# A two-layer hybrid decoder trunk: hardware loops written out, weights split ahead across the layer border, no norm prepared in the last layer, output in four blocks

## The reference

```python
for l in range(DEPTH):
    h = rms_norm(x, norm1_g[l])
    proj = h @ w_in[l]
    q, k, v, iq, ik, iw, glu_in, mq, gates = jnp.split(proj, bounds, axis=-1)
    ...
    y_attn = dsa_sparse_attention(q, k, v, iq, ik, iw) @ w_attn_o[l]
    ...
    y_mem = memory_cross_attention(mq, mk, mv) @ w_mem_o[l]
    y_conv = conformer_conv(...) @ w_conv_o[l] + conv_o_b[l]
    g = jax.nn.sigmoid(gates + gate_b[l]).reshape(B, S, N_BRANCH, D_MODEL)
    merged = g[:, :, 0] * y_attn + g[:, :, 1] * y_mem + g[:, :, 2] * y_conv
    x = x + merged @ w_out[l]
    h2 = rms_norm(x, norm2_g[l])
    x = x + jnp.square(jax.nn.relu(h2 @ w_up[l])) @ w_down[l]
return x
```

## Time and profile before

| | |
|---|---|
| median of three runs | 2966.69 us |
| the profiled execution | 2967.76 us |
| its span | 2966.1 us |
| TensorE busy | 2891.1 us |
| VectorE busy | 1745.2 us |
| ScalarE busy | 1347.8 us |
| GpSimd busy | 313.6 us |
| HBM read, written | 550.37 MB, 6.29 MB |
| mean granted TensorE clock | 0.996 of full speed |

### The profile page before, as it was taken

How to read it: one execution, slowest core, us unless ns; L and a number is a source line. 1 busy time by engine, 2 the same in 40 slices (tenths; PEclk the granted TensorE clock), 3 DMA queues, 4 the chain that set the end, 5 groups by cost and what they waited for, 6 DMA issues and landing times.

```text
span 2966.1 us, 38416 instructions
## 1 busy us (share of the span) xinstructions
PE 2891.1 (97%) x13120; PEld 2376.0 (80%) x13120; DVE 1745.2 (59%) x1849; ACT 1347.8 (45%) x1657; POOL 313.6 (11%) x331
## 2 busy tenths in 40 slices
PE   7998999999999999999999989999999999999998
PEld 6876788888888888888878768888888888888887
DVE  4689655556555555545546986555555555555554
ACT  5543644444443444444445446444444434344443
POOL 1158200000000000000020772000000000000000
PEclk9999999999999999999999999999999999999999
DMA  7653556665656556565565444666566565555653
GB/s 268 203 167 128 157 181 202 206 219 199 199 185 198 185 187 195 184 189 188 185 225 171 163 141 154 188 208 231 185 203 201 188 189 186 195 184 186 196 185 128
DMA packets 274090, 558.65 MB, mean 188 GB/s; under 512 B 13168, under 2 KB 13168, under 8 KB 271376
## 3 DMA queue, kind: packets, MB, share of 16 engines
q1 hardware_dynamic: 266384, 523.53, 53.8%
q0 software_dynamic: 5888, 30.02, 3.6%
q10 hardware_dynamic: 1664, 3.15, 0.3%
HBM read 550.37 MB, written 6.29 MB: 188 GB/s over the span
## 4 chain that ended last, share of the span: by engine, by line
PE 88%; DVE 5%; issue 4%; DMA 1%; ACT 1%; DVEq 0%; ACTq 0%; POOL 0%; POOLq 0%; SPq 0%
PE acc L548 28%; PE acc L550 28%; PE acc L549 28%; DVE conv_acc L1152 3%; PE tp L561 3%; DVE lo L1091 1%; ACT hi L818 1%; PE tp L631 1%; DMA conv_bias<-in_conv_o_b 1%; PE sc L615 0%; PE sc L604 0%; DVE index L1170 0%; DMA x_tok<-in_x 0%; DMA raw<-in_w_in 0%; DVE head_sum L1278 0%
## 5 line engine op out<-in xcount | busy, mean ns | idle before, releaser
L1091 DVE TENSOR_TENSOR lo<-raw,hi 128x1024 fp32r<-128x1024 f32 (+1 forms) x1008 | 1239.5, 1232 | 1172.4 <-ACT hi L818 1163.6
L818 ACT ACTIVATE hi<-raw 128x1024 fp32r<-128x1024 f32 (+1 forms) x1008 | 1055.6, 1048 | 1472.3 <-PE acc L550 1468.3
L548 PE MATMUL acc<-hi,hT_hi 128*128 128x512 f32 x2304 | 922.4, 400 | 37.3 <-DVE lo L1091 37.2
L550 PE MATMUL acc<-hi,hT_lo 128*128 128x512 f32 x2304 | 902.2, 392 | 0.0
L549 PE MATMUL acc<-lo,hT_hi 128*128 128x512 f32 x2304 | 901.2, 391 | 0.0
L548 PE MATMUL acc<-hi,bT_hi 128*128 128x512 f32 x1408 | 555.3, 394 | 0.0
L550 PE MATMUL acc<-hi,bT_lo 128*128 128x512 f32 x1408 | 548.9, 390 | 0.0
L549 PE MATMUL acc<-lo,bT_hi 128*128 128x512 f32 x1408 | 548.2, 389 | 0.0
L548 PEld LDWEIGHTS acc<-hi,hT_hi 128*128 128x128 f32 x2304 | 434.8, 189 | 135.6 <-DVE lo L1091 48.5
L550 PEld LDWEIGHTS acc<-hi,hT_lo 128*128 128x128 f32 x2304 | 434.6, 189 | 93.8
L549 PEld LDWEIGHTS acc<-lo,hT_hi 128*128 128x128 f32 x2304 | 435.1, 189 | 86.7
(11 more groups left out here) (224 smaller groups left out, 1641.1 us busy)
## 6 DMA issues: line engine op xcount, KB each, us to landing
raw<-in_w_in SPq DMA_DIRECT2D x160, 1024.0 KB, 5.0
raw<-in_w_up SPq DMA_DIRECT2D x128, 1024.0 KB, 5.3
raw<-in_w_down SPq DMA_DIRECT2D x128, 1024.0 KB, 5.1
raw<-in_w_out SPq DMA_DIRECT2D x32, 1024.0 KB, 5.1
raw<-in_w_mem_kv SPq DMA_DIRECT2D x16, 1024.0 KB, 5.1
raw<-in_w_attn_o SPq DMA_DIRECT2D x16, 1024.0 KB, 5.1
raw<-in_w_conv_o SPq DMA_DIRECT2D x8, 1024.0 KB, 5.0
raw<-in_w_mem_o SPq DMA_DIRECT2D x8, 1024.0 KB, 5.1
```

What stands on the lines that cost most here:

```text
L548: pe.matmul(o, a1, w1, start=first and dk == 0, stop=False)
L550: mm = pe.matmul(o, a2, w1, start=False, stop=last and dk == 1)
L818: act.activation(hi[:, u % 4, :, 0:w], raw[:, c, 2 * (u % 2):2 * (u % 2) + 2, 0:w], ACT.Copy).then_inc(hi_ready, 1)
L1091: dve.tensor_tensor(lo[:, u % 4, :, 0:w], raw[:, u // 2, 2 * (u % 2):2 * (u % 2) + 2, 0:w], hi[:, u % 4, :, 0:w].bitcast(F32), ALU.subtrac ...
```

## The change

1. Every hardware loop of the five engines is written out by the Python program. Wait values become constants; `Place` loses `base` and `loop`.
2. At the layer border VectorE no longer adds block 3 of x at the end of the layer; it adds and scales it after unit 3 of the next layer's front (n == 3), after four splits.
3. In the last layer `mlp` gets `last` as false for its last quarter too, so blocks 0 to 2 are not scaled, squared, transposed and split, and GpSimd doesn't load the gain for it.
4. The output goes in four DMAs of 512 channels, each as soon as its block is added.

```diff
-PER = {
-    "layer": {"group": GROUPS, "unit": GROUPS * UNITS, "acc0": 35, "acc1": 35, "fill": 112, "tp0": 56, "tp1": 56,
...
+A_LAYER = {"group": GROUPS, "unit": GROUPS * UNITS, "acc0": 35, "acc1": 35, "fill": 112, "tp0": 56, "tp1": 56,
...
     def now(self, name):
-        return self.base[name] + self.n[name]
+        return self.n[name]
...
-    @contextmanager
-    def loop(self, kind, i, first, trips):
...
+    def layer_done(self):
+
+        for name, per in A_LAYER.items():
+            if name not in self.counted:
+                self.n[name] += per
...
             sp.wait_ge(x_in[1], 16)
-            with sp.Fori(0, LAYERS) as l, here.loop("layer", l, 0, LAYERS):
+            for l in range(LAYERS):
...
-                with sp.Fori(0, CB) as cb, here.loop("merge", cb, 0, CB):
+                for cb in range(CB):
...
-                with sp.Fori(0, FFN // D) as qu, here.loop("ffn", qu, 0, FFN // D):
+                for qu in range(FFN // D):
...
-            sp.wait_ge(x_new, LAYERS * (CB + CB * FFN // D))
-            sp.dma_start(out_tokens.rearrange("t p d -> p t d"), x_tok[:, :, :]).then_inc(out_done, 16)
-            sp.wait_ge(out_done, 16)
+            for b in range(CB):
+                cols = slice(b * COL, (b + 1) * COL)
+                sp.wait_ge(x_new, LAYERS * (CB + CB * FFN // D) - CB + b + 1)
+                sp.dma_start(out_tokens.rearrange("t p d -> p t d")[:, :, cols], x_tok[:, :, cols]).then_inc(out_done, 16)
+            sp.wait_ge(out_done, 16 * CB)
...
@@ TensorE @@
-            with pe.Fori(0, LAYERS) as l, here.loop("layer", l, 0, LAYERS):
+            for l in range(LAYERS):
...
-                mlp(True, False)
-                with pe.Fori(1, FFN // D - 1) as qu, here.loop("ffn", qu, 1, FFN // D - 2):
-                    mlp(False, False)
-                mlp(False, True)
+                for qu in range(FFN // D):
+                    mlp(qu == 0, qu == FFN // D - 1 and l < LAYERS - 1)
+                here.layer_done()
...
@@ VectorE (ScalarE's loops are written out in the same way) @@
-            with dve.Fori(0, LAYERS) as l, here.loop("layer", l, 0, LAYERS):
+            for l in range(LAYERS):
+                layer_fill[0] = here.now("fill")
                 origin[0] = here.now("unit")
                 for n in range(FRONT * UNITS):
                     split(n % UNITS, width_of(n // UNITS))
-                    if n == 0:
+                    if n == 0 and l == 0:
+                        scale_block(CB - 1)
+                    if n == 3 and l > 0:
+                        add_block(CB - 1, 0, -1)
                         scale_block(CB - 1)
                     side(n)
...
-                mlp(False, True)
-                origin[0] = here.now("unit")
-                add_block(CB - 1, 0, -1)
+                    mlp(qu == 0, qu == FFN // D - 1 and l < LAYERS - 1)
                 here.next("rstd_ready", 2)
+                here.layer_done()
+            origin[0] = here.now("unit")
+            add_block(CB - 1, 0, -1)
...
@@ GpSimd @@
-                pool.wait_ge(scaled, here.next("scaled", T + CB))
-                alone()
-                pool.dma_start(gain[:, :], rows(norm1_g[LAYERS - 1 - l])).then_inc(gain_in, 16)
-                here.next("scaled", CB - 1)
-
-            pool.wait_ge(gain_in, here.now("gain_in"))
+                if l < LAYERS - 1:
+                    pool.wait_ge(scaled, here.next("scaled", T + CB))
+                    alone()
+                    pool.dma_start(gain[:, :], rows(norm1_g[l + 1])).then_inc(gain_in, 16)
+                    here.next("scaled", CB - 1)
+                here.layer_done()
```

More of the change, by code:

```diff
@@ L18 @@
-from contextlib import ExitStack, contextmanager
+from contextlib import ExitStack
 import numpy as np
@@ L784, in _ @@
                 merge(True)
-                with pe.Fori(1, CB) as c, here.loop("merge", c, 1, CB - 1):
+                for c in range(1, CB):
                     merge(False)
@@ L1043, in _ @@
                     take_norm(b, t)
-            with act.Fori(0, LAYERS) as l, here.loop("layer", l, 0, LAYERS):
+            for l in range(LAYERS):
                 origin[0] = here.now("unit")
@@ L1049, in _ @@
                 merge(True, 0)
-                with act.Fori(1, CB) as c, here.loop("merge", c, 1, CB - 1):
+                for c in range(1, CB):
                     merge(False, c)
@@ L1433, in _ @@
                 alone()
-                with dve.Fori(1, CB) as c, here.loop("merge", c, 1, CB - 1):
+                for c in range(1, CB):
                     origin[0] = here.now("unit")
@@ L1621, in _ @@
             here.next("scaled", CB - 1)
-            with pool.Fori(0, LAYERS) as l, here.loop("layer", l, 0, LAYERS):
+            for l in range(LAYERS):
                 pool.wait_ge(squared, here.now("squared") + T * CB)
@@ L1639, in _ @@
                         biases(l, 0)
-                with pool.Fori(1, CB) as c, here.loop("merge", c, 1, CB - 1):
+                for c in range(1, CB):
                     pool.wait_ge(bias_used, here.next("bias_used"))
```

66 lines of the change are left out of this document (20 added, 46 removed).

## The result

| | before | after |
|---|---|---|
| median | 2966.48 us (2966.23 to 2967.82, 4 runs) | 2942.98 us (2941.28 to 2944.02, 4 runs) |
| the profiled execution | 2967.76 us | 2942.02 us |
| its span | 2966.1 us | 2940.2 us |

The ratio is 0.9918, with a 95% interval of 0.9903 to 0.9933: 23.5 us faster, and the profiled executions lie 25.7 us apart. The forecast was 16.9 us and 2949.8 us, with a range down to 2946.0.

A forecast was written before the change was run, and what follows sets the result against it. TensorE, busy 97% of the span, was taken to bound the kernel. Terms 5.8 + 2.4 + 1.3 + 2.8 + 3.4 + 1.2 = 16.9 us took the median from 2966.69 to 2949.8 us, range 2946.0 to 2953.8.

The forecast's parts named there:

- Layer border, gap and clock: Between layers 0 and 1: moving VectorE's add removes TensorE's gap, 5.8 us, and the low clock behind it, 2.4 us.
- Start: Before the first matmul: ScalarE's activation table load moves to the first tanh, saving 1.3 us, bounds 0 and 1.3.
- Last layer without the norm: TensorE's last quarter: six groups of four transposes go, saving 2.8 us, bounds 2.6 and 2.9.
- Output: After the last add: only a 512 KB transfer of 3.0 us remains, saving 3.4 us, bounds 1.4 and 4.0.
- Registers gone: Mainly VectorE in the front: constant wait values shorten starts behind the top-k, saving 1.2 us, bounds 0 and 3.5.
- 0.06, times 16: VectorE in the front: 0.06 us kept per `lo` start after top-k replacement, times 16, giving 1.0 us.
- The 2 us for the clock: In the front: one clock fall more or less, 2 us either way, as part of the range.
- 1, the gap only moved: Layer border: late add and scale delay transposes or parked x, 8.2 us come back, giving 2958.0 us; 5%.
- 2, instruction supply: TensorE's longer list: instruction packets come too slowly; at 0.3 us each, 13 us slower, 2979.8 us; 3%.
- 3, little changes: Whole kernel: the border gap comes back and two more clock falls occur, saving 4.7 us, giving 2962.0 us; 2%.
- a wait for `xg`: Near the layer border: a TensorE wait for `xg` would show a forecast error.
- a pitch above 0.227: In the MLP: a pitch above 0.227 would show a forecast error.

The follow-up runs named there:

- e1: Kernel before with only VectorE's loops written out, the last x block's add left at the layer's end: 2955.66 us (before, same chip: 2967.16).
- e12: Kernel after, but VectorE's add of the last x block back at the end of layer 0, the scale after the first split: 2946.64 us.
- e2: Kernel before with only GpSimd's loops written out: 2965.17 us (before, same chip: 2967.16).
- e4: Kernel before with only the output sent in four blocks, all loops kept: 2964.07 us (before, same chip: 2967.16).
- e3: Kernel before with only ScalarE's loops written out: 2967.57 us (before, same chip: 2967.16).
- e10: Kernel after with six more semaphore increments on GpSimd, once per layer before its first convolution step: 2941.22 us.
- e11: Kernel after with one more semaphore increment on VectorE, once per layer before the first top-k round: 2941.13 us.
- e14: Kernel after, unchanged, measured again on another chip: 2940.91 us over 4 runs, ratio 0.9908 to the kernel before.
- e9: Kernel after with two more semaphore increments on GpSimd, once per layer before its first convolution step: 2941.58 us.
- e7: Kernel before with 29 of GpSimd's 30 multiply-and-add convolution steps left out: 2937.47 us (before, same chip: 2968.68).
- e8: Kernel after with 29 of GpSimd's 30 multiply-and-add convolution steps left out: 2918.50 us.
- e13: Kernel after with GpSimd's 30 convolution multiplications per layer moved to ScalarE, six buffers between: 2941.39 us over 4 runs, ratio 0.9910 to the kernel before.
- e16: Kernel after with 29 of GpSimd's 30 convolution multiplications left out, all additions kept: 2944.19 us.
- e5: Kernel after with one more semaphore increment on VectorE behind each of the eight top-k rounds: 2949.48 us.

## Why the prediction was right and wrong

**Layer border, gap and clock (5.8 + 2.4): right.** 8.1 us for 8.2. Nothing waits for the late scale, and the clock stays at 1.00. e1 and e12 split it: 5.2 by VectorE's loop written out, 2.9 by the order (4.4 with the fall in e12).

**Start (1.3, bounds 0 and 1.3): right in its mechanism, slightly too small.** 1.9 us in the profile, above the upper bound. Four runs with the old start of ScalarE and VectorE or one of them (before, e1, e2, e4) began between 22.24 and 22.94, so half a microsecond is scatter; e3, with the table load alone gone, began at 21.44. Table loads are two instead of three, as forecast.

**Last layer without the norm (2.8): right**, 2.9.

**Output (3.4): right**, 3.7. The last 512 KB took 2.75 us from the issue at 2937.06 to the landing, where I had 3.0; the whole 2048 KB had taken 6.4. (The median of all four pieces is 5.2; the other three were sent beside matmuls.) A line through 2.75 and 6.4 has a foot of 1.5 us, an estimate of what each piece pays anew. The Trainium skill (DMA: Bandwidth & Descriptors, Anatomy of one DMA, the fit) gave 3.2 as an estimate for 512 KB; its fit was measured on another kind of queue, the one that GpSimd serves. The measured value is lower, so the measurement decides.

**Registers gone (1.2, bounds 0 and 3.5): this is the step that failed.** It measured 9.4 us in units 56 to 105 of the two layers. Single profiles scatter there by 2 us with the clock, so I also took means: over before, e2, e3 and e4 the stage takes 188.8 us in either layer, over after, e10, e11, e12 and e14 184.6 and 183.6, again 9.4; with e1 and e9 it is 8.9. The direct price was sized rightly where it can be seen alone: 0.08 us less behind each round, 0.2 to 0.4 in units 72 to 87 of a layer (e7 against e8). It is a small part of the 9.4. VectorE's busy time fell by 6.0 us in the two stages (2.5 and 3.5), and that fall needs GpSimd's steps (e7 and e8 have none of it); the rest is waits and the clock, mostly in units 86 to 105, which no run takes apart. What I left out is that "0.06, times 16" was put at a point where two engines race. I took the durations of VectorE's instructions as given, and read the row as an idle time to be removed. My upper bound, all 3.5 us of that row, was a bound on idle time alone and none on the work behind it. The trace of before held the hint, in the group of `conv_acc` by tile (duration in ns: least, median, greatest):

```profile
L1152 DVE SCALAR_TENSOR_TENSOR conv_acc<-uT,tapT,conv_acc x180: 470/558/2621, 169.7 to 1775.0; 128x256 f32<-128x256 f32 x180
```

180 equal instructions, from 0.47 to 2.62 us. I never asked what made them unequal.

The Trainium skill (SBUF — State Buffer, Who interferes with whom) says that a VectorE instruction with two inputs in SBUF contends with a GpSimd instruction that reads SBUF, that the ports they share are an exclusive lock, and that the order of issue decides who blocks. The trace agrees in this: `lo` of 1.2 us takes up to 3.14, and where GpSimd is 0.1 us ahead it keeps its own duration. The wait is shorter than the other's row, though: at 235.40 `lo` overlaps a multiplication by 0.82 us and takes 0.22 longer than the one at 233.44. I had read no row in that light before predicting.

**Range.** The 2 us for the clock was about right (the falls moved, and their number changed little). No allowance was made for durations that change. With the register term at its upper bound of 3.5 us the forecast would still have been 2947.5. (4 us below 2949.8 is 2945.8, where the prediction has 2946.0; the measured time lies below both.)

**Rivals.** 1, the gap only moved: did not come, no wait near the border. 2, instruction supply: the queue has 103 packets where I took 100, and the 120 us of merge from 480 are full as before:

```profile
480.00:600.00 120.00, 120.00 (x534) 99.32 (x534) 73.56 (x66) 51.48 (x50) 3.32 (x5) 1.00 0.71 228
```

3, little changes: did not come. Of the signs I had named, the border, the order of `x_tok`, the table loads, 128 transposes of `xg` and 512 KB at the end held; the first matmul came at 20.7 for 21.3. None of the signs that I gave for an error fired (a wait for `xg`, a pitch above 0.227, more low clock). The sign that would have shown it, VectorE's own busy time in the late front, was not on my list. The terms that held did not hold by luck: e1, e3, e4 and e12 show the border, the start and the output singly.

**Open.** Why a delay in each round settles in the long pattern and its absence in the short one was not derived from the order of instructions, and e13 and e16 show that I can't predict it. Whether it must come in each round is open too, since e9 to e11 shifted nothing. That the two engines lengthen each other's instructions is shown by e5 to e8 and the rows; that it is this pair of SBUF accesses and not another shared resource is the Trainium skill's statement, which the runs agree with and don't prove.

## What to carry to other kernels

Where equal instructions on one engine have unequal durations, ask whether another engine lengthens them. Here 0.08 us at a point that repeats 8 times went with 4.7 us per layer: put that into the range, with the lengthened time in the trace as its size. Compare the busy time of a stage and not only its waits, over a stretch wide enough that no long wait crosses its border. When you put in a shift as a test, look in the trace whether the next instruction really moved. And where a hardware loop's last instruction feeds the first one of the next pass, price the branch: here writing VectorE's loop out was worth 5.2 us at one border.

## What I had not expected of the hardware

- Two instructions that start 0.01 us apart (233.43 and 233.44) took 1.96 and 1.24 us; with 0.10 us between them, the other way, 0.92 and 1.46. In e5, 0.12 us gave 0.92 and 1.43.
- One more semaphore increment on VectorE, about 0.1 us, repeated 8 times, cost 2.6 and 4.9 us in units 56 to 105 of the two layers (6.4 in units 72 to 87); two more added 0.8 and 1.4.
- Six increments on GpSimd ahead of an instruction that followed a long one cost nothing (e10).
- Taking half the steps away from GpSimd did not make VectorE faster (e16, 154.2 us busy in units 56 to 105 of layer 0 for 154.1).
- A TensorE wait of 2.8 us at the border was followed by a low clock in e12, and one of 2.7 us by none in e1.
